# A two-layer encoder on one core: score products of 32 keys in four column groups, masked scores added by GpSimd, and the order of sums in the layer norms

## The chip, the cores and the metric

The kernel runs on one core of one Trainium2 chip. The metric is device time in microseconds; times of several runs are given by their median. Engines are named as the profile names them: PE (TensorE; PEld are its weight loads), DVE (VectorE), ACT (ScalarE), POOL (GpSimd), SP (SyncE, which issues the DMAs).

## What is computed

An encoder of two layers on 512 tokens of 1024 channels, all in fp32. Each layer is: SwiGLU feed-forward, layer norm, a mixer, layer norm, SwiGLU, layer norm; shifts, scales and gates of each part come from a modulation vector (silu(c) @ ada_w). The mixer of layer 0 is a neighbourhood attention of 16 heads, that of layer 1 is a gated recurrence of 8 heads, run forwards and backwards in time, in chunks of 64 tokens. The part of the reference that the change touches most is the recurrence within a chunk:

```python
b = jnp.cumsum(g, axis=3)
b_ref = b[:, :, :, HGRN_CHUNK // 2:HGRN_CHUNK // 2 + 1]
tri = jnp.tril(jnp.ones((HGRN_CHUNK, HGRN_CHUNK), dtype=bool))
a = jnp.einsum('nbhtd,nbhsd->nbhts', q * jnp.exp(b - b_ref), k * jnp.exp(b_ref - b))
a = jnp.where(tri, a, 0.0)
o_intra = jnp.einsum('nbhts,nbhsv->nbhtv', a, v)
...
o = o_f + o_b
```

and the layer norm:

```python
mu = jnp.mean(z32, axis=-1, keepdims=True)
var = jnp.mean(jnp.square(z32 - mu), axis=-1, keepdims=True)
return ((z32 - mu) * lax.rsqrt(var + LN_EPS) * g + b).astype(out_dtype)
```

## The kernel before

Activations stay in SBUF, channels on partitions and the 512 tokens along the free axis. A projection works on units: 128 output channels, for which SP loads raw weights, ACT rounds them to w_hi (fp32r, L599), DVE forms the rest w_lo (L830), and PE runs three matmuls for each 128 input channels (L1459 to L1461: w_hi x h_hi, w_hi x h_lo, w_lo x h_hi, 512 columns each). The program is a list of phases (in and out halves of each feed-forward, `na`, `hg`, their output projections). All order is written out by hand: each engine has one instruction stream, and semaphores carry the dependencies. In `drive`, which ACT and DVE share, a step s of iteration i first converts the weights of unit (i, s) and then does the `finish` of unit (i - 1, s): what the mixer needs once that projection is there.

**The recurrence (`hg`).** A head has five projections (two forget gates, value, query, output gate). While head i is projected, PE runs the parts of head i - 1 behind them (`hgrn(j, part)`). Parts 0 and 1, one per direction d: the score product (L1713), keys kk[d] stationary, decayed queries e1[d] moving, output with keys on partitions; two chunks of 64 share a block of 128. It is made in two rounds of four matmuls, one for the 32 queries of a chunk that may see all its keys, and one for the other 32, whose keys are kk_early[d] (lg[d] reused): the half of the keys that these queries can see, with zeros in the other half, built by DVE (L982, L983). Then four transposes of kk (L1723). DVE `masked` copies the scores with a mask into am[d] (L1035), which is zero elsewhere. Parts 1 and 2: state products (L1735), from which DVE forms the states (`states`). Part 3: output into bank 7, v_tok x am[0] and v_tok x am[1], eight matmuls (L1746), and the states with qg[d] (L1754), which POOL makes in `gates` (L1407). `masked` of head j waits until PE has read the am of head j - 1 (inter_mm).

**The layer norm.** During the last output projection POOL adds the residual tiles into zsum (L1325) and DVE their squares into qsum (L890). Ahead of the last two k of the last unit PE sums both over partitions (`sums_of_seven`, by `token_sums`, L1499: four matmuls of one column, eight records). Behind the unit `statistics` runs: four matmuls of 512 columns whose output nobody reads (`keep_busy`, L1518), the sums of the eighth tile and of its square, the mean spread over partitions into bank 6 (`spread`, L1505), a filler, the reciprocal deviation spread into bank 7, nine fillers. ACT copies the mean to SBUF (L772) for POOL, which centres tiles 4 to 7; DVE centres tiles 0 to 3 (L1168) and multiplies all eight (L1175); ACT makes h_hi (L743) and h32 (L749); the next phase's `first_units` (L1474, L1475) consume h_hi tile by tile.

**The attention (`na`)** has three units a head pair: q, k, v. `scores(0)` (L1656) of the prologue waits for ACT's copy v_win (L631). The attention values (L1682) write two groups of 64 rows; the modulation sums (`reduce_ada`, L1612) write four groups of 32 rows of one bank.

## Time and profile before

| | |
|---|---|
| median of 3 runs | 2172.89 us (2172.58 to 2173.0) |
| profiled execution, own time | 2172.79 us |
| its span, first to last instruction | 2171.1 us |
| PE busy | 2134.1 us (98%) |
| DVE, ACT, POOL busy | 1214.1, 787.9, 235.6 us |
| granted PE clock, mean | 0.997 |

The span is what the trace covers; what the device time has beyond it lies around it. A matmul's record has a start and a modelled end, and records overlap, so a stretch of PE work is read from start to start. An fp32 matmul leaves two records, an fp32r one and a transpose one. In the views by order of time a row gives start, duration, engine, line, output and inputs, shapes of stationary or moving operand, how many records it merges, and in brackets the idle time before it with what ended it. In the chain a duration is the stretch from a piece's start to the next one's.

### The profile page before, as it was taken

To read this page: it belongs to the slowest core of one execution; us is meant where nothing else is said; L and a number is where in the kernel's file an instruction comes from. 1 tells how busy PE (TensorE), PEld (TensorE's weight loads), DVE (VectorE), ACT (ScalarE), POOL (GpSimd) and SP (SyncE) were. 2 spreads that over 40 slices of the span, in tenths; PEclk is the share of its full clock that TensorE was granted. 3 is DMA by queue.
4 is the path that set the end of the run, shared out by engine and by line. 5 is a ranking of instruction groups with operands and counts; after the bars stand their busy time and mean duration, and the time that the engine had idled before them with its cause. 6 is when DMAs were issued, how large, how long until landed. Compare 5 with 4: busy or idle time off the path is not lost.

```text
span 2171.1 us, 30542 instructions
## 1 busy us (share of the span) xinstructions
PE 2134.1 (98%) x10587; PEld 1756.4 (81%) x10587; DVE 1214.1 (56%) x1910; ACT 787.9 (36%) x1086; POOL 235.6 (11%) x230
## 2 busy tenths in 40 slices
PE   7999999999999999999999999999999999999997
PEld 5788888788888888888888888878888888888886
DVE  6766664655557666655535533576576555333334
ACT  4221222554444222223532222376655535322222
POOL 0000000431122000001200000241111122000002
PEclk9999999999999999999999999999999999999999
DMA  9757752243326667633236532432122123323322
GB/s 314 220 177 207 210 166 79 74 118 96 87 76 188 186 180 232 186 99 116 84 104 186 151 97 70 119 88 69 58 68 68 39 68 88 92 87 112 97 73 83
DMA packets 405669, 266.34 MB, mean 123 GB/s; under 512 B 9416, under 2 KB 366184, under 8 KB 405608
## 3 DMA queue, kind: packets, MB, share of 16 engines
q1 hardware_dynamic: 405608, 265.57, 41.1%
q8 instruction: 33, 0.54, 0.1%
q14 instruction: 28, 0.23, 0.0%
HBM read 263.37 MB, written 2.19 MB: 122 GB/s over the span
## 4 chain that ended last, share of the span: by engine, by line
PE 93%; DVE 2%; ACT 2%; issue 1%; POOL 1%; DMA 0%; SPq 0%; POOLq 0%; DVEq 0%; ACTq 0%
PE ps L1459 26%; PE ps L1461 26%; PE ps L1460 25%; PE ps L1713 1%; PE ps L1474 1%; PE ps L1475 1%; PE ps L1754 1%; PE ps L1499 1%; PE ps L1735 1%; PE ps L1656 1%; PE ps L1480 1%; PE ps L1682 1%; PE ps L1746 1%; PE ps L1667 1%; PE ps L1491 1%
## 5 line engine op out<-in xcount | busy, mean ns | idle before, releaser
L830 DVE TENSOR_TENSOR w_lo<-raw,w_hi 128x1024 fp32r<-128x1024 f32 (+2 forms) x384 | 436.0, 1136 | 748.4 <-ACT w_hi L599 748.2
L599 ACT ACTIVATE w_hi<-raw 128x1024 fp32r<-128x1024 f32 (+2 forms) x384 | 371.9, 970 | 1152.6 <-PE ps L1461 1112.2
L1459 PE MATMUL ps<-h_hi,w_hi 128*128 128x512 f32 x1744 | 689.6, 395 | 3.7 <-DVE g L839 2.2
L1461 PE MATMUL ps<-h_hi,w_lo 128*128 128x512 f32 x1744 | 679.7, 390 | 0.0
L1460 PE MATMUL ps<-h_lo,w_hi 128*128 128x512 f32 x1744 | 679.0, 389 | 0.0
L1459 PEld LDWEIGHTS ps<-h_hi,w_hi 128*128 128x128 f32 x1744 | 327.6, 188 | 80.8 <-issue 8.1
L1461 PEld LDWEIGHTS ps<-h_hi,w_lo 128*128 128x128 f32 x1744 | 327.4, 188 | 68.7
L1460 PEld LDWEIGHTS ps<-h_lo,w_hi 128*128 128x128 f32 x1744 | 327.7, 188 | 67.7 <-issue 1.4
L1459 PE MATMUL ps<-g_hi,w_hi 128*128 128x512 f32 x704 | 276.0, 392 | 0.0
L1461 PE MATMUL ps<-g_hi,w_lo 128*128 128x512 f32 x704 | 274.1, 389 | 0.0
L1460 PE MATMUL ps<-g_lo,w_hi 128*128 128x512 f32 x704 | 274.0, 389 | 0.0
L1325 POOL TENSOR_TENSOR zsum<-zsum,x 128x512 f32<-128x512 f32 x42 | 58.5, 1393 | 1440.2 <-DVE x L862 1439.6
L1459 PEld LDWEIGHTS ps<-g_hi,w_hi 128*128 128x128 f32 x704 | 132.1, 188 | 29.3 <-issue 2.4
L1461 PEld LDWEIGHTS ps<-g_hi,w_lo 128*128 128x128 f32 x704 | 132.1, 188 | 27.6
L1460 PEld LDWEIGHTS ps<-g_lo,w_hi 128*128 128x128 f32 x704 | 132.2, 188 | 26.9
L1076 DVE SCALAR_TENSOR_TENSOR acc<-ada_raw,c_silu,acc 128x512 f32<-128x512 f32 x192 | 143.6, 748 | 4.9
L612 ACT ACTIVATE sq<-x 128x512 f32 (+1 forms) x48 | 30.3, 632 | 98.3 <-DVE x L862 78.3
L843 DVE TENSOR_TENSOR g_lo<-g,g_hi 128x512 f32 (+1 forms) x88 | 61.0, 693 | 9.1
L839 DVE TENSOR_TENSOR g<-s_tmp,ps 128x512 f32<-128x512 f32 x88 | 59.9, 681 | 7.0 <-ACT s_tmp L606 6.9
L890 DVE TENSOR_TENSOR qsum<-qsum,sq 128x512 f32<-128x512 f32 x42 | 44.8, 1066 | 26.8 <-ACT sq L612 26.8
L1474 PE MATMUL ps<-h_hi,w_hi 128*128 128x512 f32 x144 | 57.5, 399 | 2.0 <-ACT h_hi L743 2.0
L1475 PE MATMUL ps<-h_hi,w_lo 128*128 128x512 f32 x144 | 56.4, 392 | 0.0
(254 smaller groups left out, 2019.0 us busy)
## 6 DMA issues: line engine op xcount, KB each, us to landing
raw<-in_ffn_w_in_dram SPq DMA_DIRECT2D x176, 512.0 KB, 3.8
ada_raw<-in_ada_w_dram SPq DMA_DIRECT2D x128, 512.0 KB, 4.3
raw<-in_ffn_w_out_dram SPq DMA_DIRECT2D x64, 384.0 KB, 3.4
raw<-in_ffn_w_out_dram SPq DMA_DIRECT2D x64, 320.0 KB, 3.1
raw<-in_hgrn_w_in_dram SPq DMA_DIRECT2D x40, 512.0 KB, 3.7
raw<-in_na_w_qkv_dram SPq DMA_DIRECT2D x24, 512.0 KB, 3.7
boot<-in_ada_w_dram SPq DMA_DIRECT2D x8, 512.0 KB, 6.9
boot<-in_ada_w_dram SPq DMA_DIRECT2D x16, 256.0 KB, 6.2
```

Of the source, the lines that this page charges most:

```text
L599: nc.scalar.activation(w_hi[s][:, 0:ph.kt, :], raw[s][:, 0:ph.kt, :], ACT.Copy).then_inc(S.w_hi_done, 1)
L830: nc.vector.tensor_tensor(w_lo[s][:, 0:ph.kt, :], raw[s][:, 0:ph.kt, :], w_hi[s][:, 0:ph.kt, :].bitcast(F32), ALU.subtract).then_inc(S.w_l ...
L839: nc.vector.tensor_tensor(g32[par][:], s_tmp[par][:], ps[:, s, :], ALU.mult).then_inc(S.pair_free, 1)
L843: nc.vector.tensor_tensor(g_lo[:, bass.ds(i * 2 + par, 1)], g32[par][:], g_hi[:, bass.ds(i * 2 + par, 1)].bitcast(F32), ALU.subtract).then ...
L890: nc.vector.tensor_tensor(qsum[:], qsum[:], sq[:], ALU.add).then_inc(S.qsum_done, 1)
L1076: nc.vector.scalar_tensor_tensor(out=acc[:, 0:width], in0=w, scalar=c_silu[:, row:row + 1], in1=acc[:, 0:width], op0=ALU.mult, op1=ALU.add ...
L1325: nc.gpsimd.tensor_tensor(zsum[:], zsum[:], x[:, bass.ds(tile, 1)], ALU.add).then_inc(S.zsum_done, 1)
L1459: nc.tensor.matmul(ps[:, bank, :], w_hi[s][:, k, :], a, start=start and k == 0, stop=False)
L1460: nc.tensor.matmul(ps[:, bank, :], w_hi[s][:, k, :], b, start=False, stop=False)
L1461: ins = nc.tensor.matmul(ps[:, bank, :], w_lo[s][:, k, :], a, start=False, stop=stop and k == ph.kt - 1)
L1474: nc.tensor.matmul(ps[:, bank, :], w_hi[s][:, at, :], h_hi[:, at, :], start=at == 0, stop=False)
L1475: nc.tensor.matmul(ps[:, bank, :], w_lo[s][:, at, :], h_hi[:, at, :], start=False, stop=False)
```

## The change

- The score product makes, for each chunk, one matmul with 32 early keys (in time order of the direction) against all 64 queries, and one with the 32 late keys against the 32 late queries. Output rows start at 0, 32, 64 or 96. That is 16 matmuls instead of 8 for each direction, 32 stationary columns instead of 128. kk_early, its two DVE instructions and its semaphore go.
- POOL adds am[0] and am[1] into am_both (`both_ways`, at the head of the next `gates`); part 3 multiplies v_tok with the sum, four matmuls instead of eight. `masked` waits for the sum of the head before.
- Layer norms 0 to 4: the sum of zsum moves from ahead of the last two k to behind the last product, in place of four fillers. The last norm (5) keeps its order.
- DVE centres tile 0 once the mean is spread, and waits for ACT's copy only behind its first multiplication; ACT copies the mean after that centring.
- In `na` ACT and DVE do a step's `finish` ahead of its conversion.

```diff
@@ -190,10 +190,10 @@
         self.gam_done = sem("gam_done")
         self.qq_done = sem("qq_done")
         self.kk_done = sem("kk_done")
-        self.early_done = sem("early_done")
         self.qg_done = sem("qg_done")
         self.a_mm = sem("a_mm")
         self.am_ready = sem("am_ready")
+        self.am_summed = sem("am_summed")
         self.kkt_mm = sem("kkt_mm")
         self.kkt_ready = sem("kkt_ready")
         self.pp_mm = sem("pp_mm")
@@ -358,6 +358,7 @@
             cum = [sb(f"cum{d}", [P, T], where=reg) for d in range(2)]
             e1 = [sb(f"e1_{d}", [P, T], where=reg) for d in range(2)]
             am = [sb(f"am{d}", [P, T], where=reg) for d in range(2)]
+            am_both = sb("am_both", [P, T], where=reg)
             st = [sb(f"st{d}", [P, NCH - 1, P], where=reg) for d in range(2)]
             gam = [sb(f"gam{d}", [P, NCH], where=reg) for d in range(2)]
             gam_t = [sb(f"gam_t{d}", [P, NCH], where=reg) for d in range(2)]
@@ -368,10 +369,6 @@
             on = h32[1]
             kk_tok = [zsum, qsum]
             qg = [sq, mean]
-            kk_early = [lg[0], lg[1]]
-
-            def half_of(tile, d):
-                return tile[:].rearrange("p (c t) -> p c t", t=CH)[:, :, d * (CH // 2):(d + 1) * (CH // 2)]
 
         def last_gain(h):
             return s_tmp[h % 2][:]
@@ -436,8 +433,12 @@
             for n, ph in enumerate(phases):
                 def steps(i):
                     for s in range(ph.body):
-                        convert(ph, i, s)
-                        finish(ph, i - 1, s)
+                        if ph.kind == "na":
+                            finish(ph, i - 1, s)
+                            convert(ph, i, s)
+                        else:
+                            convert(ph, i, s)
+                            finish(ph, i - 1, s)
                         if ride is not None and ph.ada is not None:
                             if s == 2:
                                 gather(ph, i - 1)
@@ -769,6 +770,7 @@
                 nc.scalar.activation(tok[:, 2], tok[:, 2], ACT.Sqrt).then_inc(S.sd_done, 1)
                 if n < NLN - 1:
                     act.wait_ge(S.mean_spread, n + 1)
+                    act.wait_ge(S.cent_done, DVE_CENTRED * n + 1)
                     nc.scalar.activation(mean[:], ps[:, 6, :], ACT.Copy).then_inc(S.mean_copied, 1)
                     make_h(n + 1)
                 else:
@@ -978,9 +980,6 @@
                         dve.wait_ge(S.k1_done, n + 1)
                         dve.wait_ge(S.e2_done, n + 1)
                         nc.vector.tensor_tensor(kk[d][:], kk[d][:], lg[d][:], ALU.mult).then_inc(S.kk_done, 1)
-                        dve.wait_ge(S.kk_done, n + 1)
-                        nc.vector.tensor_copy(half_of(kk_early[d], d), half_of(kk[d], d))
-                        nc.vector.memset(half_of(kk_early[d], 1 - d), 0.0).then_inc(S.early_done, 1)
                     dve.wait_ge(S.qs_done, i + 1)
                     for d in range(2):
                         n = i * 2 + d
@@ -1030,7 +1029,7 @@
                 dve.wait_ge(S.am_zero, 3)
                 dve.wait_ge(S.a_mm, n + 1)
                 if not (isinstance(j, int) and j == 0):
-                    dve.wait_ge(S.inter_mm, j * 2)
+                    dve.wait_ge(S.am_summed, j)
                 nc.vector.memset(hold[:, d:d + 1], 0.0)
                 nc.vector.copy_predicated(am[d][:].rearrange("p (a b) -> p a b", b=P),
                                           tri[d][:].rearrange("p (a b) -> p a b", a=1).to_broadcast([P, T // P, P]),
@@ -1191,10 +1190,11 @@
                     finished()
                     return
                 dve.wait_ge(S.y_read, ph.y0 + KT + 2)
-                dve.wait_ge(S.mean_copied, n + 1)
+                dve.wait_ge(S.mean_spread, n + 1)
                 centre(0)
                 dve.wait_ge(S.rstd_spread, n + 1)
                 normalise(0)
+                dve.wait_ge(S.mean_copied, n + 1)
                 for k in range(1, DVE_CENTRED):
                     centre(k)
                     normalise(k)
@@ -1388,8 +1388,16 @@
                     pool.wait_ge(S.hconst, done)
                 nc.gpsimd.memset(tri_f[:, 0:1], 0.0).then_inc(S.am_zero, 1)
 
+            def both_ways(j):
+                pool.wait_ge(S.am_ready, j * 2 + 2)
+                if not (isinstance(j, int) and j == 0):
+                    pool.wait_ge(S.inter_mm, j * 2)
+                nc.gpsimd.tensor_tensor(am_both[:], am[0][:], am[1][:], ALU.add).then_inc(S.am_summed, 1)
+
             def gates(i):
                 later = not (isinstance(i, int) and i == 0)
+                if later:
+                    both_ways(i - 1)
                 pool.wait_ge(S.ev_done, i * 5 + 4)
                 nc.gpsimd.tensor_tensor(q_raw[:], q_raw[:], q_sig[:], ALU.mult).then_inc(S.qs_done, 1)
                 pool.wait_ge(S.ev_done, i * 5 + 5)
@@ -1420,8 +1428,10 @@
                     pool.wait_ge(S.unit_done, ph.u0)
                     hgrn_constants()
                     gates(0)
-                    with pool.Fori(1, ph.iters) as i:
+                    gates(1)
+                    with pool.Fori(2, ph.iters) as i:
                         gates(i)
+                    both_ways(ph.iters - 1)
                 if ph.kind == "out" and ph.last:
                     if first:
                         restart_sums(0)
@@ -1507,8 +1517,9 @@
                 return ins
 
             def sums_of_seven(ph):
-                pe.wait_ge(S.zsum_done, ph.t0 + KT + 1)
-                token_sums(6, zsum, True)
+                if ph.ln == NLN - 1:
+                    pe.wait_ge(S.zsum_done, ph.t0 + KT + 1)
+                    token_sums(6, zsum, True)
                 pe.wait_ge(S.qsum_done, ph.t0 + KT + 1)
                 token_sums(7, qsum, True)
 
@@ -1519,7 +1530,8 @@
 
             def statistics(ph):
                 n = ph.ln
-                keep_busy(ph, 4)
+                pe.wait_ge(S.zsum_done, ph.t0 + KT + 1)
+                token_sums(6, zsum, True)
                 pe.wait_ge(S.y_read, ph.y0 + KT + 2)
                 token_sums(6, x[:, KT - 1, :], False).then_inc(S.stat_done, 1)
                 pe.wait_ge(S.sq_done, (n + 1) * KT)
@@ -1705,12 +1717,14 @@
                         pe.wait_ge(S.am_ready, n)
                     elif not first:
                         pe.wait_ge(S.am_ready, n - 1)
-                    pe.wait_ge(S.early_done, n + 1)
-                    for part_of, keys_of in ((1 - d, kk[d]), (d, kk_early[d])):
-                        for b in range(T // P):
-                            two = slice(b * P // CH, (b + 1) * P // CH)
-                            a = ps[:, bank, :].rearrange("p (c t) -> p c t", t=CH)[:, two, part_of * (CH // 2):(part_of + 1) * (CH // 2)]
-                            ins = nc.tensor.matmul(a, keys_of[:, b * P:(b + 1) * P], half_of(e1[d], part_of)[:, two, :], start=True, stop=True)
+                    half = CH // 2
+                    early, late = (0, half) if d == 0 else (half, 0)
+                    for ch in range(NCH):
+                        row, col = CH * (ch % 2), CH * ch
+                        for keys0, seen, width in ((early, 0, CH), (late, late, half)):
+                            ins = nc.tensor.matmul(ps[row + keys0:row + keys0 + half, bank, col + seen:col + seen + width],
+                                                   kk[d][:, col + keys0:col + keys0 + half], e1[d][:, col + seen:col + seen + width],
+                                                   start=True, stop=True)
                     ins.then_inc(S.a_mm, 1)
                     if d == 1:
                         pe.wait_ge(S.kkt_ready, n)
@@ -1738,13 +1752,10 @@
                 if part == 3:
                     if not first:
                         pe.wait_ge(S.n1_done, j)
-                    for d in range(2):
-                        n = j * 2 + d
-                        pe.wait_ge(S.am_ready, n + 1)
-                        for b in range(T // P):
-                            c = slice(b * P, (b + 1) * P)
-                            nc.tensor.matmul(ps[:, 7, c], v_tok[:, c], am[d][:, c], start=d == 0 and b == 0, stop=False,
-                                             skip_group_check=True)
+                    pe.wait_ge(S.am_summed, j + 1)
+                    for b in range(T // P):
+                        c = slice(b * P, (b + 1) * P)
+                        nc.tensor.matmul(ps[:, 7, c], v_tok[:, c], am_both[:, c], start=b == 0, stop=False, skip_group_check=True)
                     for d in range(2):
                         n = j * 2 + d
                         pe.wait_ge(S.qg_done, n + 1)
```

## Rows read from the trace of the kernel before

**Rows 1.** The page of the kernel before: span, busy time of each engine.

```profile
span 2171.1 us, 30542 instructions
...
PE 2134.1 (98%) x10587; PEld 1756.4 (81%) x10587; DVE 1214.1 (56%) x1910; ACT 787.9 (36%) x1086; POOL 235.6 (11%) x230
```

**Rows 2.** Who waited for whom: total us, times, longest.

```profile
PE ps L1474 <- ACT h_hi L743: 2.0, 2, 1.5
```

**Rows 3.** Busy us (x instructions) of each engine in one head of the recurrence.

```profile
1487.70:1528.20 40.50, 40.50 (x245) 34.48 (x244) 26.45 (x47) 25.03 (x34) 6.36 (x4) 1.00 0.22 65
```

**Rows 4.** Chain that ended last, in one head: start, us, what.

```profile
1487.70 1.73 PE ps L1713 x16
...
1511.06 1.78 PE ps L1746 x16
```

**Rows 5.** Order of time, PE, around one modulation sum: start, us, engine, line, tiles.

```profile
68.97 0.39 PE L1460 MATMUL ps<-h_lo,w_hi 128*128 128x512 f32 x1
69.19 0.39 PE L1461 MATMUL ps<-h_hi,w_lo 128*128 128x512 f32 x1
69.51 0.43 PE L1612 MATMUL ps<-acc_out,one 128*32 128x128 f32 x8
...
70.20 0.39 PE L1460 MATMUL ps<-h_lo,w_hi 128*128 128x512 f32 x1
```

**Rows 6.** Source line L1612, whole run: duration ns min/median/max.

```profile
L1612 PE MATMUL ps<-acc_out,one x256: 272/284/297, 69.5 to 1228.9; 128*32 128x128 f32 x128
```

**Rows 7.** Chain that ended last, in one attention head.

```profile
511.46 1.90 PE ps L1682 x32
```

**Rows 8.** The page, costliest groups: POOL's addition of 128x512.

```profile
L1325 POOL TENSOR_TENSOR zsum<-zsum,x 128x512 f32<-128x512 f32 x42 | 58.5, 1393 | 1440.2 <-DVE x L862 1439.6
```

**Rows 9.** Order of time, DVE, in the head of rows 4.

```profile
1497.64 0.73 DVE L1035 COPY_PREDICATED am<-tri,ps 128x512 f32<-128x512 uint8 x1
```

**Rows 10.** Order of time, all engines, layer norm 0.

```profile
402.81 1.13 DVE L890 TENSOR_TENSOR qsum<-qsum,sq 128x512 f32<-128x512 f32 x1 [0.80 <-ACT sq L612]
...
404.22 0.94 PE L1499 MATMUL ps<-mean_w,zsum 128*128 128x1 f32 x8
...
405.03 1.03 PE L1499 MATMUL ps<-mean_w,qsum 128*128 128x1 f32 x8
...
405.92 0.49 PE L1459 MATMUL ps<-g_hi,w_hi 128*128 128x512 f32 x1
...
407.40 1.09 PE L1518 MATMUL ps<-g_hi,w_hi 128*128 128x512 f32 x4
...
408.41 0.97 PEld L1499 LDWEIGHTS ps<-mean_w,x 128*128 128x128 f32 x8 [0.35 <-DVE x L862]
...
411.39 0.60 ACT L772 ACTIVATE mean<-ps 128x512 f32<-128x512 f32 x1 [0.32 <-PE ps L1505]
411.43 1.07 PE L1505 MATMUL ps<-ident,tok 128*128 128x128 f32 x8
...
412.88 0.69 DVE L1175 TENSOR_TENSOR x<-x,ps 128x512 f32<-128x512 f32 x1
```

**Rows 11.** Order of time, layer norm 4, ahead of the last product's end.

```profile
1782.03 0.83 DVE L890 TENSOR_TENSOR qsum<-qsum,sq 128x512 f32<-128x512 f32 x1 [0.86 <-ACT sq L612]
...
1782.37 1.05 PE L1499 MATMUL ps<-mean_w,zsum 128*128 128x1 f32 x8 [0.54 <-POOL zsum L1325]
```

**Rows 12.** Order of time, ACT and PE, prologue of the attention.

```profile
432.28 1.06 ACT L599 ACTIVATE w_hi<-raw 128x1024 fp32r<-128x1024 f32 x1 [0.66 <-PE ps L1480]
...
433.25 1.19 ACT L631 ACTIVATE v_win<-ps 128x256 f32<-128x256 f32 x4
...
434.58 2.93 PE L1656 MATMUL ps<-k_sb,q_sb 64*128 64x256 f32 x16 [2.39 <-ACT v_win L631]
```

**Rows 13.** Each engine and PEclk in stretches of the prologue of rows 12.

```profile
434.00:438.00 4.00, 3.42 (x17) 2.68 (x18) 1.16 (x5) 1.72 (x3) 3.92 (x6) 0.69 0.01 2
438.00:442.00 4.00, 4.00 (x17) 3.24 (x16) 2.91 (x17) 2.70 (x11) 1.86 (x3) 0.89 0.55 124
```

## The prediction

> **What bounds the kernel now.** I read the first lines of the page, then who waited for whom on TensorE, then the chain of waits in the recurrence, then single blocks in order of time. TensorE (PE) is busy 2134.1 of 2171.1 us [rows 1], and its waits after the boot are single events, the longest two of 2.39 and 1.5 us [rows 2, 12]. The other engines matter only where one of those events sits: in a head of the recurrence VectorE (DVE) is busy 26.45 of 40.50 us and ScalarE (ACT) 25.03, while PE has no gap [rows 3]. So the sum is made of PE time that goes away, of the few waits that move, and of the granted clock. It is made against the profiled execution: its span is 2171.1 us, its own time 2172.79 (1.7 us lie around the span), and the median of the runs, 2172.89, is the same within 0.1, so a saving counts in full.
>
> **Score products (twice a head, 16 times).** Before: 8 matmuls with 128 columns of keys and 64 of queries; an fp32 matmul leaves two records in the trace, so 16 records in 1.73 us, 0.108 each [rows 4]. After: 16 matmuls, 32 records, with 32 columns of keys each (the row block of its output is its column group), 64 query columns for the early half and 32 for the late half. The nearest rows are the four matmuls of the modulation sums, which also write four groups of 32 rows and stream 128 columns: eight records lie within 0.43 us, although one alone lasts 0.27 to 0.30 [rows 5, 6], so the groups run beside each other in two rounds. What the block costs: from the 512-column product ahead (start 69.19) to the second behind (70.20) is 1.01 us; without the block two steps of 0.23 (as 68.97 to 69.19) would lie there, so it costs 0.55. Two rounds of 128 columns are 2 x 0.11, which leaves 0.33 for getting in and out of this form. New product: 8 rounds (four matmuls of two records in each group); at 64 columns a round is half of 0.11, so 8 x 0.055 + 0.33 = 0.77 us. Upper end, if a round does not shrink with its columns: 8 x 0.11 + 0.33 = 1.21. No row shows 32 such records in a row, only eight; I stay near the four-group row, because shape and placing are the same, and add 0.08 for feeding them: **0.85**. Saving 16 x (1.73 - 0.85) = **14.1 us** (8.3 to 15.4).
>
> This takes a rule into account that speaks against the change. Row first: the longest run of narrow matmuls that the trace has, 32 records of the attention values in two groups, takes 1.90 us, 0.059 per record [rows 7]. The Trainium skill, TensorE: Matmul & The Clock Gate, section "Wait — 56ns, not 53.3ns?", says that with hardware decode off the sequencer needs about 62 ns for each matmul, and that this binds once the array's work is shorter. By that page's figure a product would be an estimated 32 x 0.062 + 0.33 = 2.3 us, dearer than now. The eight records within 0.43 us do not look like 62 ns each, but eight can have been queued. It is a rival below.
>
> **Masked scores.** Part 3 multiplied v_tok with am[0] and am[1], 8 matmuls in 1.78 us; now four with their sum: 8 x 0.89 = **7.1 us** [rows 4]. The sum is one GpSimd (POOL) addition of 128x512; the same form takes 1.39 us [rows 8]. Cover: the second mask of a head starts at 1497.64 and takes 0.73, so the sum is there by 1499.8 plus a slow POOL's extra 1 us; PE asks at 1511.06 [rows 4, 9]. If that cover were gone each head would lose up to 1.4 us. Added waits: POOL's sum waits for both masks and for the last head's reads; behind it stand this head's q gate, output gate and decayed queries, which need projections that come later than the masks. DVE's mask waits for the sum of the head before instead of PE's last read, which is earlier. PE's wait has the product's later matmuls queued behind it and is met. The two DVE instructions per direction that built kk_early go; DVE idles anyway, so 0.
>
> **Layer norms 0 to 4.** The eight records that sum zsum move from ahead of the last two k of the last product to behind it, where four 512-column fillers (0.93 us) filled the time until DVE's last residual is there: fillers from 407.40, x's sum at 408.41, released by DVE [rows 10]. The moved block is as long, 0.89 (qsum's from 405.03 to the product's next step at 405.92), so x's sum still starts 1.0 us after the last product, while the last product ends 0.89 earlier. It needs qsum then: at norm 0 qsum is added by 402.81 + 1.13 = 403.94 and PE is there at 404.2, so no wait; norms 2 and 3 have the same order. 3 x 0.89 = 2.7. At norms 1 and 4 (after a mixer) qsum ends later: 1782.03 + 0.83 = 1782.86 against PE at 1781.8 (1782.37 less the 0.54 idle) [rows 11]. So PE waits 1.1 us, then 0.9 of sums, and goes on at 1783.8 instead of 1784.2: 2 x 0.35 = 0.7. Together **3.4 us** (2.0 to 5.5: with every qsum late, or none).
>
> DVE's first centring no longer waits for ACT's copy of the mean (411.39 to 411.99), but for the spread mean, some 0.7 earlier; normalising still waits for the second spread, which ends about 412.5 instead of at 412.88 [rows 10]. So the supply of x runs 0.35 ahead. ACT's copy now waits for that centring, with the making of h behind it, and POOL's four centrings start 0.6 later; both have slack, since h needs the first normalised tile anyway. PE starts behind nine fillers in any case; only its two waits for h_hi in the midst, 2.0 us together with 1.5 the longest [rows 2], shrink by 0.35 each: **0.6 us** (0 to 0.8).
>
> **Attention, conversion behind the head's step.** In the loop PE shows no wait. Only the prologue changes: v_win was copied behind a weight conversion of 1.06 us (432.28), PE waited 2.39 us for it. Now the copy can start at 432.2, so the wait is 1.3: **1.06 us**. The conversion itself moves behind the exponents, with the load of its raw slot's next weights; their products come two units later. Right after the long wait the granted clock fell: 0.69 of full in 434 to 438 us, 0.89 in the next four, that is a stretch at the 1.2 GHz level, and (0.31 + 0.11) x 4 = 1.7 us of lost work [rows 12, 13]. The wait of 1.5 us [rows 2] left the clock at full, so a wait of 1.3 should too: another **1.7 us** (0 to 1.7).
>
> **Sum.** 14.1 + 7.1 + 3.4 + 0.6 + 1.1 + 1.7 = 28.0, so 2172.9 - 28.0 = **2145 us**.
>
> **Rivals.**
> 1. Rounds do not shrink with 64 columns (0.11 each, weight loading sets them). For it: the old product also took 0.108 per record with 64 columns as with 128 in part 3. Against: there 128 columns of weights were loaded each time, here 32. Saving 8.3 in place of 14.1: 2151.
> 2. Issue limits. 32 records at the 0.059 of the attention values are 1.9, with 0.33 makes 2.2: each product costs 0.5 more than before, 16 x 0.5 = 8 lost instead of 14 gained: 2167. Against: the eight records in 0.43 us, and that 0.059 there is explained by streaming 128 columns in two groups. This is the case of the page cited above.
> 3. The clock drops in the layer norms. Where four full-width fillers stood there are now three blocks of one-column matmuls in a row (2.7 us). If the clock halves as at 434, each of five norms pays up to 1.7: 2145 + 8.5 = 2153. Against: blocks of the same sort with fillers between left it at full everywhere.
> 4. Slower: column groups of one bank take turns on long runs, a record costing as much as a full one (0.11). Then a product is 32 x 0.11 + 0.33 = 3.9 us, 16 x 2.1 = 34 lost, less the other 13.9: 2193. It decides from 0.07 us per record, where 32 records eat all other gains. Against: [rows 5] and [rows 7] both lie below that.
> 5. The sum comes late or not at all for PE (POOL behind something not seen): 8 x 1.4 = 11 back, 2156.
>
> **How the numbers follow.** Forecast 0.55; rival 1 0.17, rival 2 0.09, rival 3 0.09, rival 4 0.03, rival 5 0.03, other mishaps 0.04. The range runs from 2140 (products at 0.77, no late qsum, the upper ends of the small terms) to 2156 (rivals 1, 3 and 5 inside); outside stay rivals 2 and 4 and sums of rivals. A measurement can tell about 0.2% (4.3 us) from no change. Slower by more: rival 4 and a share of mishaps, 0.04; within: 0.02 beside; faster 0.94.
>
> **What would show it.** Right: the chain of waits has a score product of about 0.85 us x32 and part 3 x8 at 0.89; four records of one product start together; one head lasts about 37.9 us instead of 40.5; the block ahead of the last two k has one sum; the wait before the first attention scores is 1.3 and the clock 1.00 there. Wrong: a product of 1.2 (rival 1) or 2 us and more (rivals 2, 4), a clock below 1.00 behind a norm (rival 3), PE waiting for POOL's addition (rival 5), or a wait for DVE's qsum at norms 0, 2, 3.

## The result, and the profile after

The changed kernel takes 2156.2 us (median; 2152.0 to 2157.9) against 2172.9 of the kernel before on the same chip: a ratio of 0.9915 with an interval of 0.9902 to 0.9929. The ratios here are estimates from all runs of both kernels, so they differ a little from the quotient of two medians (0.9923 here). It is faster, by about 17 us (18 by the ratio). The forecast was 28, so about three fifths came, and the median lies at the upper end of the range (2156). Two of all the runs below, one of the kernel before (8264.7 us at a clock of 0.50) and one of attn_alone (2682.2 at 0.749), were slow ones and are left out of every ratio. The profiled execution took 2157.7 with a span of 2156.0, against 2172.8 and 2171.1 before.

The page of the changed kernel, span and busy times; [rows 1] is the answer of before:

```profile
span 2156.0 us, 30858 instructions
...
PE 2112.7 (98%) x10759; PEld 1734.3 (80%) x10759; DVE 1203.2 (56%) x1878; ACT 787.7 (37%) x1086; POOL 246.7 (11%) x238
```

PE's busy time fell by 21.4 us, the span only by 15.1: there are new waits. They stand in the view of who waited for whom (changed kernel, PE; line, released by, us in total, times, longest):

```profile
PE ps L1749 <- DVE st L1049: 6.3, 7, 1.1
...
PE ps L1509 <- DVE qsum L892: 2.2, 2, 1.1
...
PE ps L1668 <- ACT v_win L632: 1.4, 1, 1.4
PE ps L1725 <- DVE am L1034: 0.9, 1, 0.9
...
PE ps L1484 <- ACT h_hi L744: 0.5, 1, 0.5
```

The first line is what the prediction did not have: PE waits for the states of the recurrence, once a head from the second on (1.0 to 1.1 us in five heads, 0.2 and 0.5 in the first and the last of the seven). In the trace of before that line is

```profile
PE ps L1735 <- DVE st L1050: 0.5, 1, 0.5
```

The qsum waits came as forecast (2 x 1.1; before, PE waited 2 x 0.5 for zsum at the same two norms). The wait for the first mask at the last head (L1725, 0.9) is new as well. The wait for h_hi fell from 2.0 [rows 2] to 0.5, and the one for v_win from 2.4 to 1.4.

**Where the 15.1 us come from.** Comparing the starts of the same PE blocks in the two traces, in order of time:

| stretch | forecast us | measured us |
|---|---|---|
| five norms, to the first step of h | -3.4 | +7.2 |
| behind norm 0, to the first scores (waits for h_hi and v_win) | -1.1, and a part of -0.6 | -2.2 |
| first scores, the half clock of [rows 13] gone | -1.7 | -1.6 |
| behind norm 3 (wait for h_hi) | a part of -0.6 | -1.3 |
| recurrence: products | -14.1 | -16.3 |
| recurrence: part 3 | -7.1 | -7.1 |
| recurrence: new waits and what lies round them | 0 | +7.1 |
| all else | 0 | -0.9 |

**The product.** Changed kernel, PE, in order of time (start, us, engine, line, tiles, count), from the unit ahead to the state product behind; then the same stretch of before:

```profile
1525.98 0.39 PE L1471 MATMUL ps<-h_hi,w_lo 128*128 128x512 f32 x1
1526.30 0.65 PE L1725 MATMUL ps<-e,zt 128*32 128x64 f32 x32
1526.88 0.66 PE L1737 MATMUL ps<-ident,zt 128*128 128x128 f32 x4
1527.46 1.16 PE L1749 MATMUL ps<-h,zsum 64*128 64x128 f32 x16
```

```profile
1535.44 0.39 PE L1461 MATMUL ps<-h_hi,w_lo 128*128 128x512 f32 x1
1535.66 1.00 PE L1713 MATMUL ps<-e,zt 128*128 128x64 f32 x8
...
1537.39 0.61 PE L1723 MATMUL ps<-ident,zt 128*128 128x128 f32 x4
1537.93 1.16 PE L1735 MATMUL ps<-h,zsum 64*128 64x128 f32 x16
```

32 records take 0.58 us from start to start (1526.30 to 1526.88), 0.018 each, where 16 took 1.73. It is entered 0.32 instead of 0.22 to 0.23 us after the start of the last 512-column step, and the transposes behind it take 0.58 instead of 0.54, so 0.14 is paid for the change of form. Last unit to state product is 1.48 against 2.49. A product costs 0.72, not 0.85.

Part 3 is x8 in 0.88 (1542.10 to 1542.98), as forecast:

```profile
1542.10 1.05 PE L1758 MATMUL ps<-am_both,h 128*128 128x128 f32 x8
1542.98 1.67 PE L1765 MATMUL ps<-sq,st 128*128 128x64 f32 x14
```

**The new wait.** The second state product of the same head, DVE first, then POOL and PE (changed kernel, order of time):

```profile
1530.28 0.73 DVE L1034 COPY_PREDICATED am<-tri,ps 128x512 f32<-128x512 uint8 x1
...
1530.90 0.53 DVE L994 TENSOR_SCALAR f_sig<-f_sig,lb 128x512 f32<-128x512 f32 x1
1531.47 1.40 DVE L999 TENSOR_SCALAR zt<-f_sig 128x512 f32<-128x512 f32 x1
...
1533.11 2.27 DVE L1049 SCALAR_TENSOR_TENSOR st<-st,gam,ps 128x128 f32<-128x128 f32 x6
```

```profile
1531.09 1.50 POOL L1395 TENSOR_TENSOR am_both<-am 128x512 f32<-128x512 f32 x1 [4.58 <-DVE am L1034]
```

```profile
1533.90 0.39 PE L1471 MATMUL ps<-h_hi,w_lo 128*128 128x512 f32 x1
1535.43 1.16 PE L1749 MATMUL ps<-h,qsum 64*128 64x128 f32 x16 [1.14 <-DVE st L1049]
```

And DVE and PE in the same head of before:

```profile
1539.91 0.43 DVE L1000 TENSOR_SCALAR zt<-f_sig 128x512 f32<-128x512 f32 x1
...
1540.57 2.26 DVE L1050 SCALAR_TENSOR_TENSOR st<-st,gam,ps 128x128 f32<-128x128 f32 x6
...
1544.69 1.16 PE L1735 MATMUL ps<-h,qsum 64*128 64x128 f32 x16
```

DVE forms the states of direction 0 out of psum, and they free the place into which the next state product writes. Before, they ended at 1542.83 and PE came at 1544.69: 1.9 us of slack. Now they end at 1535.38 and PE could have gone on at 1534.2. Two things can have eaten the slack: PE comes earlier in its shorter head, and the one-input DVE instruction L999 takes 1.40 instead of 0.43 us, beside POOL's new addition (1531.09 to 1532.59). This is not one case: the 16 instructions of this line took 6.8 us before (L1000) and take 13.6 now, seven of them 1.40 and nine 0.43. The experiments below part the two.

**The norms.** Stretches around norm 0 of the changed kernel (PE, PEld, DVE, ACT, POOL busy; then PEclk, the granted clock as a share of 2.4 GHz):

```profile
406.00:410.00 4.00, 3.94 (x33) 3.73 (x33) 1.41 (x5) 0.65 (x2) 0.00 (x0) 1.00 0.46 98
410.00:414.00 4.00, 4.00 (x19) 3.60 (x18) 2.27 (x5) 1.50 (x3) 1.91 (x2) 0.57 1.02 293
```

In 410 to 414 the clock was at 1.2 GHz for about 3.4 us, 1 us behind the blocks of one-column matmuls (zsum, x and its square) that now follow each other. PE in order of time:

```profile
404.22 0.95 PE L1509 MATMUL ps<-mean_w,qsum 128*128 128x1 f32 x8
...
406.51 0.95 PE L1509 MATMUL ps<-mean_w,zsum 128*128 128x1 f32 x8
407.52 1.05 PE L1509 MATMUL ps<-mean_w,x 128*128 128x1 f32 x8
...
412.18 3.10 PE L1529 MATMUL ps<-g_hi,w_hi 128*128 128x512 f32 x9
415.11 0.39 PE L1484 MATMUL ps<-h_hi,w_hi 128*128 128x512 f32 x1
```

The sum of x starts 0.9 earlier than in [rows 10] (407.52 for 408.41), as forecast; but the nine fillers then take 2.93 us instead of 2.22, and the first step of h comes at 415.11, 0.63 later than before. All five norms of this execution show such a stretch. In norm 4 it is about 10.2 us long (12 us at 0.57), and it begins ahead of the blocks in a row, 1 us after the sum of qsum, for which PE had waited 1.1 us: the product step at 1765.69 already takes 0.63 us, and the sum of zsum starts only at 1766.54.

```profile
1764.00:1776.00 12.00, 12.00 (x56) 11.45 (x57) 4.46 (x10) 2.58 (x5) 0.80 (x1) 0.57 0.31 90
```

```profile
1765.69 0.63 PE L1470 MATMUL ps<-ohg_lo,w_hi 128*128 128x512 f32 x1
```

### The profile page after: what moved, and what is told of

Read it like the earlier page. It is cut to its first block and busy times, and to the rows that moved or that the text cites. A ratio compares the mean times of both kernels' runs of the same rounds, so it can differ in the third digit from the quotient of the medians.

```text
span 2156.0 us, 30858 instructions
## 1 busy us (share of the span) xinstructions
PE 2112.7 (98%) x10759; PEld 1734.3 (80%) x10759; DVE 1203.2 (56%) x1878; ACT 787.7 (37%) x1086; POOL 246.7 (11%) x238
```

## Experiments

The kernels come in three groups in the order of the text, each on a chip of its own beside runs of the kernel before: the first four (before: 2173.4), the next four (2172.4), the last four (2174.1). Ratios are against the kernel before of the same group, so kernels of different groups are compared by ratio.

### Which part brings what

**norm_alone**: the kernel before, with only the new order of the norm's sums.

```diff
-                pe.wait_ge(S.zsum_done, ph.t0 + KT + 1)
-                token_sums(6, zsum, True)
+                if ph.ln == NLN - 1:
+                    pe.wait_ge(S.zsum_done, ph.t0 + KT + 1)
+                    token_sums(6, zsum, True)
...
-                keep_busy(ph, 4)
+                pe.wait_ge(S.zsum_done, ph.t0 + KT + 1)
+                token_sums(6, zsum, True)
```

> The kernel before with only the norm's sums moved: zsum's sum behind the last product in place of the four fillers (norms 0 to 4), nothing else. Theory (the fillers kept the clock up): a stretch at half clock in each of the five norms, as in the changed kernel; it takes off 3.4 us by the shorter PE order and puts back 1.5 us at norms 0 to 3 and 4.5 at norm 4, so about 2180 us, 7 slower than before. Rival (the drops come from the changed kernel's shorter recurrence or attention shifting all that follows): no new stretch at half clock, about 2169.5 us.

Measured: 2174.0, ratio 0.9997 (0.9986 to 1.0009). Alone it brings nothing, neither the 3.4 of the forecast nor the loss of 7; the profiled execution, with the lowest clock of the ten (0.992), took 2179.5. The granted clock of its ten runs was 0.992 to 0.995, that of before in most runs 0.997 to 0.999. In its profiled execution four of the five norms have a half clock. Norm 0 kept its clock and shows what the order is worth by itself: from the start of the first sum to the first step of h it takes 9.34 us (404.61 to 413.95), where the kernel before takes 10.26 and the changed kernel 10.89. That is 0.9 less, as forecast. Norm 1, a stretch of 4 us:

```profile
652.00:656.00 4.00, 4.00 (x20) 4.00 (x21) 0.35 (x3) 1.57 (x2) 0.00 (x0) 0.50 1.01 332
```

**attn_alone**: the kernel before, with only the attention's new order.

```diff
-                        convert(ph, i, s)
-                        finish(ph, i - 1, s)
+                        if ph.kind == "na":
+                            finish(ph, i - 1, s)
+                            convert(ph, i, s)
+                        else:
+                            convert(ph, i, s)
+                            finish(ph, i - 1, s)
```

> The kernel before with only the attention's step order changed (finish ahead of conversion on ScalarE and VectorE). Theory: the wait before the first scores falls from 2.4 to 1.3 us and the stretch at half clock behind it is gone: 2.7 us less, 2170 us. Rival: the clock still drops there, 2172 us, which the timing can't tell from before, but the profile can.

Measured: 2171.2, ratio 0.9989 (0.9977 to 1.0001). The wait for v_win is 1.4 and no half clock follows it; its 2.2 us are at the edge of what the runs can tell. The shorter wait is the order's doing, the clock not surely so: norm_alone and rec_alone keep the old order and wait 2.4 us, and their clock stayed at full as well. In rec_alone (PE in order of time, then busy times and PEclk of the stretch):

```profile
434.11 2.00 PE L1660 MATMUL ps<-k_sb,q_sb 64*128 64x256 f32 x16 [2.39 <-ACT v_win L628]
```

```profile
434.00:438.00 4.00, 3.89 (x24) 3.24 (x25) 1.38 (x9) 1.27 (x1) 3.92 (x6) 1.00 0.01 2
```

**rec_alone**: the changed kernel with norm sums, mean and attention in the order of before.

> The kernel before with only the recurrence changed (products of 32 keys, GpSimd's sum, four matmuls in part 3). Theory: 16 products save 1.0 us each, part 3 saves 8 x 0.89 us, and the second state product of six heads waits about 1.2 us for VectorE's first states, 6.2 us in all, so 17 us less than before, 2156 us, clock as before. If the wait were a matter of the changed norms or attention, it would be absent here: 2150 us.

Measured: 2157.3, ratio 0.9917 (0.9893 to 0.9942): the recurrence alone brings all of the gain that can be measured, 16 us. The wait for the states is there in full:

```profile
PE ps L1741 <- DVE st L1044: 6.3, 7, 1.1
```

**norm_back**: the changed kernel with the norm sums and their four fillers as before; the new order of the mean stays.

> The changed kernel with only the norm's sums and the four fillers put back as they were. Theory (fillers keep the clock up): none of the five stretches at half clock is left, about 10.6 us come back and 3.4 us of shorter order are lost, so about 7 us below the changed kernel, 2148 to 2150 us. Rival: the stretches stay, then it is 3.4 us slower than the changed kernel, 2158 to 2160 us.

Measured: 2157.1, ratio 0.9915 (0.9889 to 0.9941), the ratio of the full change. The time is near the rival's 2158 to 2160, but the stretches did not all stay, as the rival has it, nor all go, as the theory has it: two norms have a half clock instead of five (one of them 8 us behind norm 3, after a wait of 1.9). PE's wait for h_hi is back, 2.1 us in two waits, the longest 1.9. At norm 3 the conversion of weights ahead of the tile it waits for took

```profile
1409.98 2.04 DVE L832 TENSOR_TENSOR w_lo<-raw,w_hi 128x1024 fp32r<-128x1024 f32 x1
```

where the same line takes 1.2 alone, and 1.57 at this place in rec_attn, which has the old order of the mean. So a norm that keeps its clock pays part of that back by reaching h before it is ready.

**rec_attn**: as norm_back, and the order of the mean as before too.

> The changed kernel with the norms wholly as before (zsum's sum, four fillers, and the order of ScalarE's mean copy and VectorE's first centring); beside norm_back it differs in the mean's order alone. Forecast's theory: the mean's new order is worth 0.6 us, so this is 2157.7 us. Rival (GpSimd's later centring falls on VectorE's weight conversion, 2.04 us in norm_back against 1.58 before, and eats the gain): TensorE's waits for h_hi are 2.0 us together, as in norm_back, and the time is the same or up to 1 us less, 2156 to 2157 us.

Measured: 2159.3, ratio 0.9938 (0.9922 to 0.9955), above both expectations. This is 5 us worse than the full change by ratio, though the intervals overlap, and should have been equal to rec_alone less 2. PE's waits for h_hi are 2.0 us together, against 2.1 in norm_back. Its clock was 0.995 in all four runs, that of rec_alone 0.997 to 0.998, though both have the norms of before: in its profile norm 1 and norm 4 (10.2 us) ran at half clock. The clock falls in norms of the old order too, only less often.

### What makes PE wait for the states

**sum_later**: POOL's addition waits until the states of direction 0 are formed.

```diff
                 pool.wait_ge(S.am_ready, j * 2 + 2)
+                pool.wait_ge(S.st_done, j * (2 * (NCH - 1)) + NCH - 1)
```

> The changed kernel, but GpSimd adds the two masked scores only when VectorE's seven states of direction 0 are there. Theory A (the new wait before the second state product comes half from GpSimd's addition, beside which VectorE's next instruction took 1.40 us instead of 0.43, half from VectorE reaching the head's work later in a shorter head): the wait falls from 1.2 to about 0.2 us a head, 5 us in all, 2151 us; TensorE still finds the sum in time (there at 6 us before it is asked for). Rival (VectorE's order alone makes it late): the wait stays at 1.2 us and the time at 2156 us.

Measured: 2152.1, ratio 0.9897 (0.9877 to 0.9917). L999 is back at 0.43, the wait at 0.16:

```profile
1534.54 0.43 DVE L999 TENSOR_SCALAR zt<-f_sig 128x512 f32<-128x512 f32 x1
...
1535.20 2.27 DVE L1049 SCALAR_TENSOR_TENSOR st<-st,gam,ps 128x128 f32<-128x128 f32 x6
...
1538.63 1.61 DVE L1012 TENSOR_TENSOR lg<-cum 128x512 f32<-128x512 f32 x1
```

```profile
1537.54 2.14 POOL L1396 TENSOR_TENSOR am_both<-am 128x512 f32<-128x512 f32 x1 [7.97 <-DVE st L1049]
```

```profile
1537.52 1.16 PE L1750 MATMUL ps<-h,qsum 64*128 64x128 f32 x16 [0.16 <-DVE st L1049]
```

(The fences are DVE, POOL and PE in order of time.) Nothing but the place of POOL's addition was changed, and the waits for the states fell from 6.3 to 1.2; PE waits once, 0.2 us, for the addition. The slowing moved with it: now L1012 takes 1.61 instead of 0.69, where nobody waits for it. The Trainium skill, SBUF — State Buffer, section "Who interferes with whom", says that DVE and GpSimd share one pair of ports as an exclusive lock, which a DVE instruction needs in its two-port modes (`tensor_scalar` has one) or, against a GpSimd instruction that reads, with two inputs in SBUF, and that in a two-port mode the engine that issues second is blocked for the whole instruction of the first. L999 ended 0.28 after POOL's addition; a whole wait would leave 0.43, so the trace agrees nearly.

**states_first**: DVE forms the states of direction 0 ahead of `forget` of direction 1.

```diff
                     if later:
                         masked(i - 1, s)
+                        if s == 1:
+                            states(i - 1, 0)
                     forget(i, s)
                 if s == 1:
-                    if later:
-                        states(i - 1, 0)
                     decay(i, 0)
```

> The changed kernel, but VectorE makes the states of direction 0 ahead of the next head's forget gate of direction 1 (0.5 + 0.4 to 1.4 us of work) instead of behind it. Theory A: the states are ready 1 to 1.9 us earlier, before TensorE asks, so the wait of 1.2 us a head is gone (6 us in all, 2150 us). Rival (TensorE's wait is bound by the state product and seven states in a row, 2.6 us, whatever comes before): 2155 us. A loss could come from the forget gate's logarithm 2.5 us later, if some later wait of the head appears.

Measured: 2149.8, ratio 0.9889 (0.9872 to 0.9905), against 0.9915 of the change. One wait of 0.5 is left, the one that before has too, and the second state product starts 0.32 behind the unit with no wait (DVE, POOL and PE in order of time):

```profile
1534.80 2.27 DVE L1049 SCALAR_TENSOR_TENSOR st<-st,gam,ps 128x128 f32<-128x128 f32 x6
```

```profile
1534.67 1.29 POOL L1395 TENSOR_TENSOR am_both<-am 128x512 f32<-128x512 f32 x1 [4.59 <-DVE am L1034]
```

```profile
1537.47 0.39 PE L1471 MATMUL ps<-h_hi,w_lo 128*128 128x512 f32 x1
1537.79 1.16 PE L1749 MATMUL ps<-h,qsum 64*128 64x128 f32 x16
```

The expectation came true. POOL's addition now lies wholly beside the states, and these take 2.27 us as ever: these instructions, whose new input lies in psum, are not slowed.

**sum_split**: the new product, but no addition by POOL; part 3 multiplies am[0] and am[1] in eight matmuls as before.

> The changed kernel without GpSimd's addition: part 3 again in eight matmuls from both masked scores. Part 3 costs 8 x 0.89 = 7.1 us more; if theory A holds, the wait before the second state product falls from 1.2 to about 0.2 us in five or six heads, 5 us back, so the sum's net worth as the kernel stands is only about 2 us: 2158 us. Rival (the wait is not of the addition's making): 2163 us.

(VectorE's masks wait for PE's last read again, as before.) Measured: 2157.1, ratio 0.9938 (0.9917 to 0.9958). Its waits for the states are 1.2 us, those of sum_later, although it has no addition at all. So 1.2 is what is left with a shorter head alone (0.5 of it, at the last head, is in the kernel before too), and the other 5.1 come of the addition. From one second state product to the next, that is for a head, it takes 38.7 us here and 38.8 with the sum: as the change places it, the sum of the masked scores gives 0.89 a head and takes the same back. Placed behind or beside the states it keeps it (37.8 and 37.6). The ratio is 5 us worse than that of the change, but the intervals overlap, and in the profiled executions sum_split is the shorter by 2 us at a higher clock (0.995 to 0.993); so the heads in the traces carry this reading.

### The clock in the norms, and the best form

All four are states_first with one more edit.

**fill_five**: `keep_busy(ph, 9)` becomes `keep_busy(ph, 5)`.

> states_first with five instead of nine fillers of 512 columns behind the second spread in each norm. Theory (where the clock is halved over the last part of a norm, each filler takes twice its 0.23 us and pushes the first product behind the time at which h_hi is ready): up to 4 x 0.43 = 1.7 us less at each norm that runs at half clock, at most 1.5 of it worth anything, and 0 at a norm at full clock, where TensorE then waits 0.9 us for h_hi instead; 4 to 7 us in all if the drops stay as long as they are, 2143 to 2146 us. Rival (fewer full-width matmuls keep the clock down longer, into the first products): no gain or a loss, 2150 us and more.

**fill_behind**: four fillers again, behind the sum of zsum.

```diff
                 token_sums(6, zsum, True)
+                keep_busy(ph, 4)
                 pe.wait_ge(S.y_read, ph.y0 + KT + 2)
```

> states_first with the four fillers put back behind the sum of zsum, so that the three blocks of one-column matmuls are broken up, but at the price of 0.9 us a norm. Theory (it is the missing fillers in that stretch that let the clock fall): no drop in norms 0, 2 and 3, 1.5 us each back, less 0.9 each: 2148 us, mean clock 0.996 and more. Rival (the place of the sum, behind the product, does it, or the wait for VectorE's qsum at norms 1 and 4): the drops stay, 4.5 us slower, 2154 us.

**sf_norm_old**: sums, fillers and mean of the norms all as before.

> states_first with the norms wholly as before. Beside states_first it prices the norm part in the better recurrence: if it is neutral, as norm_alone and norm_back showed (its 3.4 us of shorter order given back by the clock), 2150 us, within 2 us of states_first. Forecast's theory: 4 us slower, 2154 us.

**sf_mean_old**: only the mean's order as before.

> states_first with the mean's order as before (VectorE's first centring behind ScalarE's copy), all else the same. Forecast's theory: 0.6 us slower. With the clock halved over the second spread, normalising waits for that spread anyway, so the earlier centring is worth nothing: no difference that can be measured, 2150 us.

| kernel | median us | ratio (interval) | clock of its runs |
|---|---|---|---|
| fill_five | 2147.0 | 0.9876 (0.9861 to 0.9891) | 0.994 to 0.995 |
| sf_mean_old | 2147.9 | 0.9878 (0.9863 to 0.9893) | 0.994 to 0.997 |
| fill_behind | 2154.0 | 0.9906 (0.9891 to 0.9922) | 0.994 to 0.997 |
| sf_norm_old | 2153.4 | 0.9908 (0.9894 to 0.9921) | 0.993 to 0.997 |

fill_five lies between its theory and its rival, with four waits for h_hi of 3.0 us together; fill_behind has the time of its rival and, in the profile, the clock of its theory; sf_norm_old is 4 us slower than states_first, as by the forecast's theory, but with overlapping intervals; for sf_mean_old no difference was expected and none can be told.

Norm 0, PE in order of time; first fill_five, whose clock is at half in it, then fill_behind, whose clock is full:

```profile
403.50 0.95 PE L1509 MATMUL ps<-mean_w,qsum 128*128 128x1 f32 x8
...
411.63 1.97 PE L1529 MATMUL ps<-g_hi,w_hi 128*128 128x512 f32 x5
413.61 0.50 PE L1484 MATMUL ps<-h_hi,w_hi 128*128 128x512 f32 x1
```

```profile
404.22 0.95 PE L1509 MATMUL ps<-mean_w,qsum 128*128 128x1 f32 x8
...
407.32 1.16 PE L1529 MATMUL ps<-g_hi,w_hi 128*128 128x512 f32 x4
...
412.06 2.31 PE L1529 MATMUL ps<-g_hi,w_hi 128*128 128x512 f32 x9
414.21 0.39 PE L1484 MATMUL ps<-h_hi,w_hi 128*128 128x512 f32 x1
```

From the sum of qsum to the first step of h it is 10.1 us in the one and 10.0 in the other, and 10.9 in the changed kernel; norm 0 of states_first, which kept its clock without the four fillers, takes 9.3. In the profiled execution of fill_behind the clock stayed up through all five norms (it fell once, 8 us behind norm 3); but the four fillers cost 0.7 us each time whether it would have fallen or not, and the other three runs had a clock of 0.994 and took 2153.5 and more. So no gain from fillers in this place is seen: fill_behind is not better than states_first, and worse than fill_five. fill_five is the fastest of all: 27 us below before, some 9 below the change by ratio. Whether its four fillers less or only states_first makes that can't be told from 0.9889 and 0.9876, whose intervals overlap.

Norms with a half clock in them or within 10 us behind them, counted in the profiled executions: new order of the sums without fillers 27 of 35 (seven kernels), old order 8 of 30 (six kernels, the kernel before among them with none), fill_behind 1 of 5. The norms are not alike. At norms 2 and 3 it is 14 of 14 against 1 of 12, so there the new order and the half clock go together. At norm 0 it is 2 of 7 against 0 of 6. At norms 1 and 4, where PE waits for the first sum in either order (0.5 or 1.1 us), it is 11 of 14 against 7 of 12, and the traces can't tell the two orders apart. The three at norm 3 of norm_back, fill_five and fill_behind begin 8 us behind the first step of h and after a wait of 1.9 to 2.0 us for h_hi; they are of another kind. Without them it is 13 of 14 against 0 of 12 at norms 2 and 3.

## Why the prediction was right, and where it was wrong

**Products: right, and mis-sized.** The groups run beside each other and the rounds shrink with their columns, so rival 1 (1.21), rival 2 (2.2) and rival 4 (3.9) all fall by the same row: 32 records in 0.58. The term was 0.85 and measured 0.72. Its parts were off both ways: eight rounds at 0.055 + 0.08 would be 0.52 and took 0.58, but getting in and out costs 0.14, not 0.33. That 0.33 came from the modulation sum [rows 5], a short block of eight records. That such a block also pays the length of its last matmul, which a long block spreads, would explain it; no run shows it. The saving is 16.3 instead of 14.1. The Trainium skill, TensorE: Matmul & The Clock Gate, section "Wait — 56ns, not 53.3ns?", has about 62 ns for each matmul with hardware decode off. It did not bind here: 18 ns for a record, 36 for a matmul of two.

**Masked scores: right on PE, wrong on the way there.** Part 3 gave 7.1 as forecast and PE waits nowhere for the addition: rival 5 fell in the form in which it was put. But the price of the addition was asked only of the one who waits for its result. The step that failed is the sentence that the cover hides it; it had to be read for who runs beside it as well. The trace of before did have the row: POOL's additions of L1407 run beside w_lo there, which then takes 1.96 instead of 1.23 us. The 5.1 us lost that way are the larger part of the miss in the recurrence.

**The waits for DVE at nothing: the second failed step.** The prediction let the other engines matter only where a wait already stood, had none in a head ("while PE has no gap") and put DVE at 0 ("DVE idles anyway"). DVE is idle a third of a head [rows 3], but not where it matters: it works through two masks, two `forget` and the states in a row, and PE needed the states 1.9 us after they were ready. The prediction shortened PE's head by 2.65 us and did not ask which of DVE's answers was due within that time. sum_split (head shorter by 2.0 us) and sum_later (by all of the 2.65) both price this alone at 1.2 us in all, 0.7 more than before; states_first brings it back to the 0.5 of before. With states_first a head takes 37.6 us, near the 37.9 of the forecast, and 38.8 in the change.

**Norm sums: the order was right, the clock was wrong.** Counted from the product step ahead of the first sum, the first spread starts 0.90, 0.37, 0.89 and 0.90 us earlier at norms 0 to 3, the forecast of 0.89 and 0.35, and PE waits for qsum at norms 1 and 4 alone, 1.1 us each, as worked out from [rows 10, 11]. Then the half clock puts the first step of h back by 1.52 to 1.54 us at each of the four, and by some 4.5 at norm 4. That is rival 3, whose sign (a clock below 1.00 behind a norm) was named. It had the mechanism and a price of up to 1.7 a norm, but 0.09 of the chance. The reason against it, that blocks of this sort with fillers between left the clock at full, was about a state that the edit removes, and so no reason. A stretch can also last three times as long, which the price left out; at norm 4 it began ahead of the blocks in a row, so what set it off there stays open. All in all 10.6 us, of which about 1.5 come back as shorter waits for h_hi.

How much the new order of the sums is worth in the median stays open. Pairs that differ in it give: nothing (norm_alone to before, norm_back to the change), 5.5 us by the medians and 6.5 by ratio (sf_norm_old to sf_mean_old, which differ in the sums alone, with intervals that just do not overlap). In single norms the traces show both sides: 0.9 us gained where the clock holds, 0.6 lost where it is at half for 3.4 us. The clock of single runs moves by as much: two runs of before with 0.999 and 0.994 took 2170.8 and 2180.0, that is 1.8 us for each 0.001 of the mean clock. Why rec_alone kept 0.998 and rec_attn did not, with the same norms, isn't explained.

**Mean's order: not seen.** 0.6 was forecast, as shorter waits for h_hi. sf_mean_old and states_first are alike within their intervals (0.9878 and 0.9889), and the waits themselves did not shrink: 2.1 us in norm_back with the new order, 2.0 in rec_attn with the old.

**Attention: the wait right, the clock in part luck.** The wait fell by 1.00, from 2.39 to 1.39 (forecast 1.06), and the half clock behind it is gone, 1.6 us. But the prediction tied that half clock to the wait of 2.39, and norm_alone and rec_alone have the same wait at full clock. So the 1.7 us are not what the new order saves in every run. PE in the changed kernel, and the stretch that answers to the first of [rows 13]:

```profile
432.98 2.00 PE L1668 MATMUL ps<-k_sb,q_sb 64*128 64x256 f32 x16 [1.39 <-ACT v_win L632]
```

```profile
434.00:438.00 4.00, 4.00 (x24) 3.14 (x21) 2.15 (x12) 0.42 (x2) 3.66 (x6) 1.00 0.14 27
```

The sum was 28.0, the two traces differ by 15.1. Products give 2.2 more; the waits in the recurrence cost 7.1 and the norms' clock 10.6; shorter waits for h_hi and small stretches give back some 2.6 beyond the forecast. That the time still came to the end of the range is in part luck: the range was made wide for rivals 1, 3 and 5, and what filled it was rival 3, dearer than priced, and a wait that no rival had.

## What to carry to other kernels

When an edit shortens the bounding engine's loop, list for every answer it takes from the others how long before the need it is ready, and compare the shortest slack with the gain: the mean idle share of an engine says nothing of it. An instruction given to GpSimd is priced twice, once for who waits for it and once for the VectorE instruction that runs beside it; put it beside VectorE work that was seen not to slow, here the states, which read psum. And before blocks of one-column matmuls are moved together, count the clock as a term of the sum and not as a remote rival.

## What the hardware did that was not expected

- Fp32 matmuls of 32 keys in four column groups follow each other at 18 ns per record, over 32 records in a row. Changing into this form and out of it cost 0.14 us in all.
- A one-input fp32 VectorE instruction of 128x512 (0.43 us) takes up to 1.40 beside a GpSimd addition, a two-input one (0.69) 1.61; the six instructions of the states, with one input in psum, take 2.27 beside it as without it.
- TensorE's clock fell to 1.2 GHz behind one-column matmuls though PE was busy 3.94 of the 4.00 us ahead of it (norm 0), for about 3.4 us; at norms 1 and 4, where PE had waited 0.5 to 1.1 us for a sum, it was 10.2 us in some kernels. The mean clock differs from run to run of the same kernel (0.994 to 0.999 for the kernel before).
- After the same wait of 2.39 us before the attention scores the clock fell to 0.69 of full over 4 us in the kernel before and stayed at 1.00 in norm_alone and rec_alone.
